# Ordering a core's small TensorE products by array tile, and padding 16- and 32-row products to 128 rows

## The reference, cut to what matters

```python
# GLA, per head and chunk
attn = einsum('bnihk,bnjhk->bnhij', q * exp(b - b_ref), k * exp(b_ref - b)); attn = where(causal, attn, 0)
kv = einsum('bnjhk,bnjhv->bnhkv', k * exp(b_last - b), v)
log_a = log_sigmoid(ga @ gla_w_alpha + gla_b_alpha) / 16        # rank 16
# HGRN2, per head and chunk
scores = einsum('bnrhk,bnshk->bnhrs', q_dec, k_inv); scores = where(causal, scores, 0)
state = d_n[..., None] * state + einsum('brhk,brhv->bhkv', k_n, v_n)
# Mamba-2, per head and chunk
seg = a_cum[:, :, :, None] - a_cum[:, :, None, :]; l_mat = exp(where(causal, seg, -inf))
u = einsum('bnjgs,bnjghp->bnghps', bc, xc * decay_to_end)
```

## Time and profile before

| | |
|---|---|
| median of 3 runs | 1750.38 us (1750.24 to 1752.63) |
| the profiled execution | 1751.12 us, span 1749.3 us |
| granted clock over the span | 0.998 |
| PE | 1734.1 us busy, 99% |
| PEld | 1530.1 us, 87% |
| DVE | 1159.8 us, 66% |
| ACT | 729.4 us, 42% |
| POOL | 14.5 us, 1% |
| DMA | 153.82 MB, mean 88 GB/s |

### The profile page before, as it was taken

One profiled execution on the slowest core, in us unless ns is written; L12 is line 12 of the kernel. 1 busy time (PEld: TensorE's weight loads), 2 busy tenths in 40 slices (PEclk: granted clock), 3 DMA queues, 4 the chain that ended last, 5 costly groups with the idle time before them and its releaser, 6 DMA issues.

```text
span 1749.3 us, 27505 instructions
## 1 busy us (share of the span) xinstructions
PE 1734.1 (99%) x11080; PEld 1530.1 (87%) x11080; DVE 1159.8 (66%) x1796; ACT 729.4 (42%) x1119; POOL 14.5 (1%) x18
## 2 busy tenths in 40 slices
PE   9999999999999999999999999999999999999998
PEld 7888887788888888888899999999998999999887
DVE  5766656566568777734476766778788877777332
ACT  6444433332353333333545454554554433333221
POOL 0000000000000000000000000000000000000000
PEclk9999999999999999999999999999999999999999
DMA  5222332223333333333222222222222233323331
GB/s 193 85 78 79 90 95 81 85 75 96 96 97 97 96 97 96 108 98 97 77 81 73 61 73 70 65 73 73 73 61 73 85 97 97 97 88 94 103 98 64
DMA packets 45773, 153.82 MB, mean 88 GB/s; under 512 B 6064, under 2 KB 8496, under 8 KB 45648
## 3 DMA queue, kind: packets, MB, share of 16 engines
q1 hardware_dynamic: 44816, 151.29, 28.7%
q10 hardware_dynamic: 832, 0.79, 0.1%
HBM read 149.96 MB, written 2.10 MB: 87 GB/s over the span
## 4 chain that ended last, share of the span: by engine, by line
PE 92%; DVE 4%; ACT 1%; issue 1%; DVEq 1%; ACTq 0%; DMA 0%; POOL 0%; SPq 0%; POOLq 0%
PE ps L713 91%; PE ps L717 2%; DVE arena L1539 2%; ACT arena L1115 1%; DVEq L2116 1%; DVE w_lo L1536 0%; DVE arena L1546 0%; DVE h_res L1536 0%; DVE arena L1553 0%; ACTq L1519 0%; DMA h_res<-xT 0%; DVE arena L1542 0%; DVE u_lo L1774 0%; POOL ffn L693 0%; ACT w_hi L1115 0%
## 5 line engine op out<-in xcount | busy, mean ns | idle before, releaser
L713 PE MATMUL ps<-u_hi,w_hi 128*128 128x258 f32 (+3 forms) x2376 | 638.9, 322 | 1.4 <-DVE h_res L1536 1.4
L713 PE MATMUL ps<-u_lo,w_hi 128*128 128x258 f32 (+3 forms) x2376 | 633.5, 320 | 0.8 <-DVE u_lo L1774 0.8
L713 PE MATMUL ps<-u_hi,w_lo 128*128 128x512 f32 (+3 forms) x2352 | 625.7, 319 | 0.0
L1536 DVE TENSOR_TENSOR w_lo<-w_raw,w_hi 128x1024 fp32r<-128x1024 f32 (+1 forms) x279 | 340.2, 1219 | 147.9 <-ACT w_hi L1115 135.8
L713 PEld LDWEIGHTS ps<-u_hi,w_hi 128*128 128x128 f32 (+1 forms) x2376 | 394.3, 188 | 41.0 <-issue 5.1
L713 PEld LDWEIGHTS ps<-u_lo,w_hi 128*128 128x128 f32 (+1 forms) x2376 | 391.6, 187 | 34.2 <-DVE u_lo L1774 1.6
L1115 ACT ACTIVATE w_hi<-w_raw 128x1024 fp32r<-128x1024 f32 (+1 forms) x281 | 294.2, 1047 | 301.5 <-PE ps L713 294.7
L713 PEld LDWEIGHTS ps<-u_hi,w_lo 128*128 128x128 f32 x2352 | 389.4, 188 | 31.2 <-issue 0.2
L1546 DVE SCALAR_TENSOR_TENSOR ffn<-full,par,ffn 128x512 f32<-128x512 f32 (+2 forms) x176 | 132.2, 751 | 80.9 <-ACT ffn L1115 77.7
L1115 ACT ACTIVATE ffn<-full,par 128x512 f32<-128x512 f32 x88 | 67.7, 770 | 264.4 <-DVE full L1539 264.4
L1115 ACT ACTIVATE arena<-arena 128x528 f32<-128x528 f32 (+10 forms) x189 | 96.2, 531 | 167.9 <-DVE arena L1539 88.4
(11 more groups left out here) (159 smaller groups left out, 1517.1 us busy)
## 6 DMA issues: line engine op xcount, KB each, us to landing
w_raw<-weights SPq DMA_DIRECT2D x278, 512.0 KB, 3.5
h_res<-xT SPq DMA_DIRECT2D x8, 256.0 KB, 5.1
outT<-h_res SPq DMA_DIRECT2D x4, 256.0 KB, 2.2
cst<-consts SPq DMA_DIRECT2D x1, 730.0 KB, 8.2
w_raw<-weights SPq DMA_DIRECT2D x2, 256.0 KB, 4.0
outT<-ffn ACTq DMA_DIRECT2D x2, 256.0 KB, 2.5
seg<-consts SPq DMA_DIRECT2D x1, 256.0 KB, 8.1
outT<-h_res SPq DMA_DIRECT2D x2, 128.0 KB, 2.5
```

Of the source, the lines that this page charges most:

```text
L713: return nc.tensor.matmul(out, lhsT, rhs, start=start, stop=stop)
L1536: return V.tensor_tensor(out, a, b, op)
```

## The change

It does four things in the PE block, and clears what these need:

1. `head_a` of GLA: all four 128-column products first, then all 64-column ones, then the transposes into bank 5, then those into bank 6. `head_a` of HGRN2: the sixteen score products, the meta score product, then all transposes by bank.
2. `pre`, `head_b`, `head_c`, `ssm_b`, `ssm_c`: the products over 16 or 32 rows take all 128, the rows below being zero.
3. `ssm_a`: both `pick` products take 128 rows (the constant now is zero from row 32 on, so only the first stack counts), and those for the meta tokens 128 stationary columns in place of 16.
4. The zeros: POOL clears rows 32 to 127 of `wal` and `ga_sb` at the start (PE's first `pre` waits for `padded`), and `h_ktm`, `h_vtm` and `ac_st` in `second_zeros`; DVE clears `m_btm`, `m_xtm`, `m_atm` in `ssm_zero`.

```diff
+            for rows in (slice(2 * GLA_RANK, 4 * GLA_RANK), slice(4 * GLA_RANK, P)):
+                nc.gpsimd.memset(wal[rows, :], 0.0)
+                last = nc.gpsimd.memset(ga_sb[rows, :], 0.0)
+            last.then_inc(padded, 1)
...
+                    pe.wait_ge(padded, 1)
...
-                mm(ps[:, 7, :], wal[0:2 * GLA_RANK, n * P:(n + 1) * P], ga_sb[0:2 * GLA_RANK, :]).then_inc(pa_ok, 1)
+                mm(ps[:, 7, :], wal[:, n * P:(n + 1) * P], ga_sb).then_inc(pa_ok, 1)
...
+                    for at in starts:
                         mm(ps[:, 4, at:at + c], kf1[:, at:at + BLK], qf1[:, at:at + c])
+                    for b, at in enumerate(starts):
                         mm(ps[0:c, 4, at + c:at + BLK], g_kL[:, b, :], g_qB[:, b, :])
                         mm(ps[c:BLK, 4, at + c:at + BLK], kf1[:, at + c:at + BLK], qf1[:, at + c:at + BLK])
+                    for b, at in enumerate(starts):
                         turn(ps[:, 5, at:at + BLK], g_kZ[:, b, :])
+                    for at in starts:
                         last = turn(ps[:, 6, at:at + BLK], vf1[:, at:at + BLK])
...
-                    mm(ps[:, 7, 272:400], h_ktm[0:META, :], h_vtm[0:META, :])
+                    mm(ps[:, 7, 272:400], h_ktm, h_vtm)
...
-                    last = mm(ps[:, 7, 400:416], h_vtm[0:META, :], h_am[0:META, :])
+                    last = mm(ps[:, 7, 400:416], h_vtm, h_am)
...
+                every = [pick[:, 2 * t + i:2 * t + i + 1].broadcast_to((P, P)) for i in range(2)]
                 for i in range(2):
-                    rows, h = slice(32 * i, 32 * i + 2 * M2_H), 2 * t + i
-                    mm(ps[:, 4 + i, :], pick[rows, h:h + 1].broadcast_to((2 * M2_H, P)), ac_st[rows, META:T2])
+                    mm(ps[:, 4 + i, :], every[i], ac_st[:, META:T2])
                 for i in range(2):
-                    rows, h = slice(0, 2 * M2_H), 2 * t + i
-                    mm(ps[0:META, 7, 16 * i:16 * i + 16], pick[rows, h:h + 1].broadcast_to((2 * M2_H, META)),
-                       ac_st[rows, 0:META])
+                    mm(ps[:, 7, 16 * i:16 * i + 16], every[i], ac_st[:, 0:META])
...
-                mm(ps[:, 7, 160:288], m_btm[0:META, g, :], m_xtm[0:META, 1, :])
+                mm(ps[:, 7, 160:288], m_btm[:, g, :], m_xtm[:, 1, :])
...
-                    last = mm(ps[rows, 7, 288:304], m_xtm[0:META, 0, rows], m_atm[0:META, i, :])
+                    last = mm(ps[rows, 7, 288:304], m_xtm[:, 0, rows], m_atm[:, i, :])
```

More of the change, by code:

```diff
@@ L553, in program @@
         dve_chain, act_chain, zeroed = sem("dve_chain"), sem("act_chain"), sem("zeroed")
-        cleared = sem("second_cleared")
+        cleared, padded = sem("second_cleared"), sem("gla_padded")
         sq_ok, sq_added, sum_ok, rstd_ok = sem("sq_ok"), sem("sq_added"), sem("sum_ok"), sem("rstd_ok")
@@ L699, in second_zeros @@
                 nc.gpsimd.memset(h_attn, 0.0)
+                nc.gpsimd.memset(h_ktm, 0.0)
+                nc.gpsimd.memset(h_vtm, 0.0)
+                nc.gpsimd.memset(ac_st[:, :].bitcast(F32), 0.0)
                 nc.gpsimd.memset(h_am, 0.0).then_inc(cleared, 1)
+            for rows in (slice(2 * GLA_RANK, 4 * GLA_RANK), slice(4 * GLA_RANK, P)):
+                nc.gpsimd.memset(wal[rows, :], 0.0)
+                last = nc.gpsimd.memset(ga_sb[rows, :], 0.0)
+            last.then_inc(padded, 1)
             for kind, i in STEPS:
@@ L889, in head_a @@
                     pe.wait_ge(cst_in, 48)
[L890 to L893, removed]
+                starts = [b * BLK for b in range(NBLK)]
+                if gla:
+                    c = GLA_C
+                    for at in starts:
                         mm(ps[:, 4, at:at + c], kf1[:, at:at + BLK], qf1[:, at:at + c])
+                    for b, at in enumerate(starts):
                         mm(ps[0:c, 4, at + c:at + BLK], g_kL[:, b, :], g_qB[:, b, :])
                         mm(ps[c:BLK, 4, at + c:at + BLK], kf1[:, at + c:at + BLK], qf1[:, at + c:at + BLK])
+                    for b, at in enumerate(starts):
                         turn(ps[:, 5, at:at + BLK], g_kZ[:, b, :])
+                    for at in starts:
                         last = turn(ps[:, 6, at:at + BLK], vf1[:, at:at + BLK])
-                    else:
+                else:
+                    for b, at in enumerate(starts):
                         for c in range(SUB):
@@ L902, in head_a @@
                             mm(ps[HG_C * c:n_k, 4, at:at + n_k], qd2[:, q0:q0 + HG_C], KC[:, b, c * BLK:c * BLK + n_k])
+                    mm(ps[0:META, 7, 0:16], kcm[:, 0, :], qd2[:, 0:META])
+                    for b, at in enumerate(starts):
                         turn(ps[:, 5, at:at + BLK], KC[:, b, SUB * BLK:(SUB + 1) * BLK])
-                        last = turn(ps[:, 6, at:at + BLK], vf2[:, META + at:META + at + BLK])
-                if not gla:
-                    mm(ps[0:META, 7, 0:16], kcm[:, 0, :], qd2[:, 0:META])
+                    for at in starts:
+                        turn(ps[:, 6, at:at + BLK], vf2[:, META + at:META + at + BLK])
                     turn(ps[0:META, 7, 16:144], kcm[:, 1, :])
@@ L2037, in ssm_zero @@
                 V.memset(m_cbm, 0.0)
+                V.memset(m_btm, 0.0)
+                V.memset(m_xtm, 0.0)
+                V.memset(m_atm, 0.0)
             def ssm_bc(g):
@@ L2127, in constants @@
     rows = np.arange(P)[:, None]
-    c[:, 384:400] = rows % M2_H == np.arange(M2_H)[None, :]
+    c[:, 384:400] = (rows % M2_H == np.arange(M2_H)[None, :]) & (rows < 2 * M2_H)
     c[:, 400:401] = -1.0 * (rows % 32 >= M2_H)
```

## The result

| | before | after |
|---|---|---|
| median of the runs | 1750.41 us (1750.24 to 1752.63) | 1735.13 us (1734.9 to 1735.65) |
| the profiled execution, its span | 1751.12, 1749.3 us | 1735.65, 1733.9 us |
| ratio of the times | | 0.991, 95% interval 0.9893 to 0.9927 |
| granted clock over the span | 0.998 | 0.998 |

The account below looks back on a forecast made before the run. PE, busy 99% of the span, was taken to bound the kernel, with crossings between tile shapes as the price; 8.8 + 3.0 + 2.4 + 3.0 + 1.6 + 1.7 = 20.5 us less gave 1730 us, range 1726.5 to 1734.5 us.

Parts of the forecast that it names:

- HGRN2 `head_a`, 8.8 us: Eight stages, scores grouped ahead of the transposes: from 3.18 us to 2.09 us, 1.1 us less each, 8.8 us in all.
- rival 1: HGRN2 `head_a`: the narrow score stream keeps 0.35 us a block, 3.1 us less gain, 1733 us; 10%.
- rival 4: HGRN2 `head_a`: the sixteen scores queue for their strips, a head takes 7.5 us, 1773 us in all, slower; 2%.
- The HGRN2 heads have room: HGRN2 heads: DVE busy 21.8 of 31.1 us, no PE waits in middle heads, so PE's cuts there count in full.
- Rival 2: HGRN2: a chain over DVE and ACT holds the head at, say, 30.5 us; 1.2 us of 8 heads lost, 1740 us; 4%.
- `head_b`, 3.0 us: Eight HGRN2 stages, rows padded to 128: 1.54 us becomes 1.24 us, entry 0.09 us less; 0.38 us each, 3.0 us.
- `head_c`, 2.4 us: Eight HGRN2 stages, last product over the whole array: 0.77 us becomes 0.47 us; 0.30 us each, 2.4 us.
- GLA `head_a`, 3.0 us: Four GLA stages, products grouped by shape: 3.13 us becomes 2.38 us; 0.75 us each, 3.0 us.
- `pre`, 1.6 us: Four stages, two passes over the whole array: 1.05 us plus 0.09 us of entry becomes 0.69 us; 0.39 us each, 1.6 us.
- Mamba, 1.7 us: Mamba stages `ssm_a`, `ssm_b`, `ssm_c`: PE alone would give 3.2 us, waits for DVE leave 1.7 us.
- widening `ssm_a`: Eight Mamba stages, lost overlap of two 512-column products: 0.1 us dearer each, 0.8 us.
- Rival 3: All padded stages: rows make no crossing, padding brings nothing, only the order gains and `ssm_a` loses its overlap; 1740 us; 3%.

Follow-up runs that it names:

- experiment 1: The changed kernel with only the HGRN2 `head_a` put back into its old order, transposes between the blocks of scores: 1739.93 us.
- experiment 5: The changed kernel with both `head_a` back in their old order, so padding and the wider `ssm_a` alone: 1744.95 us (1742.82 to 1745.91 us).

## Why the prediction was off

- **HGRN2 `head_a`, 8.8 us.** The stage gained 1.1 us as forecast, so the term of PE's work is right to 0.2 us, and rival 1 (a slower narrow stream) is out: a further block costs 0.22 us. So is rival 4 (scores queuing), which wanted a longer stream. What reached the end is less; experiment 1 measures it in place at 4.8 us.
- **The step that failed** is the sentence "The HGRN2 heads have room": "PE waits at none of the middle heads, and each chain from one stage to the next spans a projection group, which doesn't shrink". No wait means only that the slack isn't negative. It was 1.2 us, and readable: ACT's copies ended 1.2 us ahead of `head_b` before the change. "Middle heads" also leaves out the first, where PE already waited 0.2 us for this chain. And the chain that ends in these copies doesn't start at `head_a`. It spans `head_c`, `head_d` and `head_a` of PE, which shrink by 0.3 and 1.1 us between them, more than the slack. DVE's 9.3 us of idle time a head were pieces in this chain, not room.
- **Rival 2** was this mechanism (a chain over DVE and ACT holds the head back; I gave it 4%). Its period of 30.5 us was somewhat too long: the distances from one `head_a` to the next are 30.8 us for the first head and 29.5 to 30.1 us for the next six, and were 31.1 us (31.3 us for the first, 30.5 us for the last). The loss against a pure stream is 4.0 us in the starts of seven `head_b` and 0.1 us more in the length of each, 0.7 us, together 4.7 us; 0.2 us of it was there before.
- **`head_b`, 3.0 us.** 0.38 us where PE doesn't wait, right; in seven of eight heads the wait took it.
- **`head_c`, 2.4 us.** 0.31 us for seven heads, right (the timeline has 1.92 us where it had 2.20 us); 0.1 us for the eighth. The seventh's gain went into the wait for `v_lo` at the next `head_d` (1.1 to 1.4 us).
- **GLA `head_a`, 3.0 us.** 0.73 us each, 2.9 us: right.
- **`pre`, 1.6 us.** 0.41 us each for three heads, right. The first kept only 0.1 us: GLA's first `head_a`, 17 us on, comes 29.26 us after the first norm where it came 29.38 us after it. The trace shows where the rest went. In between, PE needs the `w_lo` of a new slab. Before, DVE ended it at 45.95 us, 0.3 us ahead of the first product behind it (46.25 us). After, DVE ended it at 46.37 us, 0.42 us later, about as much as the first norm stood later (0.44 us), and that product stands at 46.47 us, 0.40 us behind its neighbour where the pace is 0.23 us. The products around it hold PE busy, so the list of waits doesn't show it. All ten profiled kernels with the padded `pre` have these 0.4 us, the two without it don't: the step that failed in HGRN2, on a small scale. The late start takes 0.3 us net of this 0.1 us.
- **Mamba, 1.7 us.** 2.2 us. `ssm_b` gained 0.38 us and `ssm_c` 0.15 us with its entry, both near the forecast; widening `ssm_a` cost half of what I took. The waits for DVE grew by 1.7 us, from 3.9 to 5.6 us by the lists of PE's waits (forecast 1 to 1.5 us). After:

```profile
PE ps L720 <- DVE h_res L1549: 2.4, 4, 1.4
PE ps L720 <- DVE arena L1552: 2.0, 2, 1.3
PE ps L720 <- DVE v_lo L2122: 0.7, 1, 0.7
PE ps L720 <- DVE arena L1566: 0.5, 1, 0.5
```

- **Rival 3** (rows make no crossing) is out: `head_b` and `ssm_b` lost 0.38 us by their rows alone. The rule of the Trainium skill named with it ("TensorE: Matmul & The Clock Gate", Part 3 on products side by side, and the table in "Why this matters for your kernels" on the time of one) agrees with the trace on the overlap: the two products over 32 rows start together in `ssm_a` before. It prices no change of shape, and by it padding would have gained nothing, where experiment 5's trace gained 8.45 us.
- **The sum**, by stages that count: 9.5 (HGRN2) + 2.9 + 1.2 + 2.2 - 0.3 = 15.5 us, the difference of the two profiled executions. With ACT's copies ahead of its tanh the kernel takes 1730.6 us; the forecast of 1730 us is what PE's list alone would give.
- **The range** was built from the bounds of PE's prices only. A wait that isn't in the list before had 4% and lay outside it.

## What to carry to other kernels

When a change shortens the busiest engine, "it waits nowhere" is no measure of room: at each of its waits read how long before it the releaser had finished, and compare that slack with the sum of all cuts inside the releaser's chain, which can be several stages long. An in-order engine that serves two consumers should do first what the bound engine waits for; here two calls moved in ACT's order were worth 4.5 us, where the whole change brought 15.3 us. And group small products by tile shape: the bank they write made no difference, the shape 1.1 us a stage.

## What the runs showed of the hardware that was not expected

- A stretch of small products that starts after a wait costs 0.10 us more than one that follows the projection products at once, beside the wait itself (`head_b` 1.35 against 1.25 us). The kernel before doesn't show it: its `head_b` takes 1.54 us with and without a wait ahead, so a change of shape at the start seems to hide it. In both cases the time lies between the first two passes, which start 0.21 us apart in place of 0.11 us.
- A stream of products with 32 stationary columns, sixteen in a row over four strips, keeps 0.11 us a pass of the widest strip. The starts of the single passes show that the strips run apart: the one with 32 moving columns takes a pass each 0.03 to 0.09 us and starts its eighth at 0.32 us, the one with 128 at 0.81 us. The 16-column meta product, last of the scores in program order, starts at 0.49 us, ahead of passes issued before it.
- Widening a product's rows from 16 or 32 to 128 with zeros costs PE nothing by itself (the widened passes of `head_b` start 0.11 us apart like all others) and saves 0.38 us where it keeps a stage in one shape. Giving up the overlap of two 512-column products for it is about even (0.055 us dearer a stage).
- The products of 256 and 258 columns can run 1% slower for a whole network at the same granted clock and with no wait, 2.2 us here (seen in one profile). A change of a few us is better read from stages than from a median over few runs.
